# Gate and up columns of an expert's stage moved by one matmul over two runs of 256 columns

## The reference

```python
for e in range(N_EXPERTS):                       # 8
    ye = swiglu(xt, wg[e], wu[e], wd[e])         # (silu(x @ wg) * (x @ wu)) @ wd
    out = out + ye * gates[:, e:e + 1]           # gates: softmax over the top 2, else 0
```

## Time and profile before

| what | value |
| --- | --- |
| median of the timed executions | 1815.68 us (1813.15 to 1816.01) |
| the profiled execution, first to last instruction | 1820.0 us |
| TensorE busy with matmuls | 1738.7 us, 96% |
| VectorE busy | 1251.5 us, 69% |
| ScalarE busy | 983.8 us, 54% |
| mean granted clock of TensorE | 0.954 of full |
| expert part, first stage to last | about 751 to 1805 us |
| load of 1 MB, issue to landing, median | gate 5.2, up 5.3, down 5.0 us |

### The profile page before, as it was taken

How to read it: one execution, slowest core, us unless ns; L and a number is a source line. 1 busy time by engine, 2 the same in 40 slices (tenths; PEclk the granted TensorE clock), 3 DMA queues, 4 the chain that set the end, 5 groups by cost and what they waited for, 6 DMA issues and landing times.

```text
span 1820.0 us, 28008 instructions
## 1 busy us (share of the span) xinstructions
PE 1738.7 (96%) x11045; PEld 1521.8 (84%) x11053; DVE 1251.5 (69%) x1280; ACT 983.8 (54%) x1013; POOL 59.7 (3%) x54
## 2 busy tenths in 40 slices
PE   7998699999899998899999999999999999999998
PEld 5774369999639847899899999899999999999997
DVE  4256655555526543788688888788888888888885
ACT  3344434443145502487577566676676666676664
POOL 0132000000100030100000000000000000000000
PEclk9997589999989999799899999999999999999998
DMA  7321024566204403499899999999999998998993
GB/s 245 93 93 47 1 93 134 167 204 212 93 0 129 148 1 116 139 366 329 282 361 324 324 363 315 327 361 315 332 362 313 335 361 301 349 362 295 352 361 126
DMA packets 335774, 429.10 MB, mean 236 GB/s; under 512 B 9491, under 2 KB 305817, under 8 KB 335409
## 3 DMA queue, kind: packets, MB, share of 16 engines
q1 hardware_dynamic: 332216, 423.77, 69.1%
q10 hardware_dynamic: 3512, 4.73, 0.8%
HBM read 427.43 MB, written 1.05 MB: 235 GB/s over the span
## 4 chain that ended last, share of the span: by engine, by line
PE 84%; DVE 5%; DMA 5%; ACT 3%; issue 2%; SPq 0%; DVEq 0%; ACTq 0%
PE ps L1397 82%; DMA raw<-in_moe_w_up_dram 3%; PE ps L1409 2%; ACT w_hi L825 1%; DMA ring<-in_ffn_w_down_dram 1%; DVE ring_lo L1075 1%; DMA raw<-in_moe_w_down_dram 1%; DVE arena L1021 0%; DVE xg_lo L1330 0%; ACT arena L556 0%; DVE arena L914 0%; DMA arena<-in_meta_tokens_dram 0%; ACT ring_hi L713 0%; DVE arena L1146 0%; SPq L469 0%
## 5 line engine op out<-in xcount | busy, mean ns | idle before, releaser
L1215 DVE TENSOR_TENSOR w_lo<-raw,w_hi 128x2048 fp32r<-128x2048 f32 x336 | 760.9, 2287 | 167.8 <-ACT w_hi L825 164.7
L825 ACT ACTIVATE w_hi<-raw 128x2048 fp32r<-128x2048 f32 x336 | 633.1, 1912 | 29.7 <-DMA raw<-in_moe_w_down_dram 16.2
L1397 PE MATMUL ps<-w_hi,xg_hi 128*128 128x256 f32 x1792 | 517.5, 289 | 2.6 <-DVE xg_lo L1330 2.6
L1397 PE MATMUL ps<-w_hi,xg_lo 128*128 128x256 f32 x1792 | 506.8, 283 | 0.0
L1397 PE MATMUL ps<-w_lo,xg_hi 128*128 128x256 f32 x1792 | 506.8, 283 | 0.0
L1397 PEld LDWEIGHTS ps<-w_hi,xg_hi 128*128 128x128 f32 x1792 | 342.5, 191 | 9.0 <-issue 3.7
L1397 PEld LDWEIGHTS ps<-w_lo,xg_hi 128*128 128x128 f32 x1792 | 343.2, 192 | 3.7
L1397 PEld LDWEIGHTS ps<-w_hi,xg_lo 128*128 128x128 f32 x1792 | 342.7, 191 | 0.0
L850 ACT ACTIVATE eh_hi<-ps 128x256 fp32r<-128x256 f32 x112 | 43.2, 386 | 278.1 <-PE ps L1409 278.1
L1397 PE MATMUL ps<-w_hi,eh_hi 128*128 128x512 f32 x448 | 179.2, 400 | 1.0 <-DVE eh_lo L1302 1.0
L1397 PE MATMUL ps<-w_lo,eh_hi 128*128 128x512 f32 x448 | 177.0, 395 | 0.0
(11 more groups left out here) (244 smaller groups left out, 1954.9 us busy)
## 6 DMA issues: line engine op xcount, KB each, us to landing
raw<-in_moe_w_gate_dram SPq DMA_DIRECT2D x112, 1024.0 KB, 5.2
raw<-in_moe_w_up_dram SPq DMA_DIRECT2D x112, 1024.0 KB, 5.3
raw<-in_moe_w_down_dram SPq DMA_DIRECT2D x112, 1024.0 KB, 5.0
ring<-in_w_in_ab_dram SPq DMA_DIRECT2D x12, 1024.0 KB, 5.4
ring<-in_hy_w_in_dram SPq DMA_DIRECT2D x12, 1024.0 KB, 5.1
ring<-in_ffn_w_gate_dram SPq DMA_DIRECT2D x11, 1024.0 KB, 5.4
ring<-in_ffn_w_up_dram SPq DMA_DIRECT2D x11, 1024.0 KB, 5.4
ring<-in_ffn_w_down_dram SPq DMA_DIRECT2D x8, 1408.0 KB, 7.0
```

What stands on the lines that cost most here:

```text
L825: nc.scalar.activation(w_hi[:, p, at, :], raw[:, p, at, :], ACT.Copy).then_inc(sem(f"{part}_high"), 1)
L1215: V.tensor_tensor(w_lo[:, p, at, :], raw[:, p, at, :], w_hi[:, p, at, :].bitcast(F32), ALU.subtract).then_inc(sem(f"{part}_split"), 1)
L1397: return nc.tensor.matmul(o, l, r, start=start, stop=stop)
```

## The change

`columns`, which did gate or up, gives way to `gate_up(n, p, part)`. One matmul now moves 256 gate columns and the 256 up columns of the same row block, which lie 2048 elements apart in `w_hi` and `w_lo`, and writes all 512 columns of the PSUM bank. Part 0 does the first four of the eight row blocks, part 1 the last four. The turn of the stage before stays in the middle, now between the two parts. Part 0 waits for both `g_split` and `u_split`. One semaphore `gu_used` is raised at the end of part 1, where there were `g_used` after gate and `u_used` after up; the loads of gate and of up, and the silu, wait for it.

```diff
-                    sp.wait_ge(sem(f"{part}_used"), 14 * i + 2 * q + p - 1)
+                    sp.wait_ge(sem("d_used" if part == "d" else "gu_used"), 14 * i + 2 * q + p - 1)
...
             def silu(n, p):
-                act.wait_ge(sem("u_used"), n + 1)
+                act.wait_ge(sem("gu_used"), n + 1)
...
-            def columns(part, n, p):
-
-                pe.wait_ge(sem(f"{part}_split"), n + 1)
-                at = "gud".index(part)
-                w = [a[:, p, at, :].rearrange("p (k n) -> p k n", k=KT) for a in (w_hi, w_lo)]
-                for k in range(KT):
-                    last = product(ps[p][:, 256 * at:256 * at + 256], xg_hi[:, k, :], xg_lo[:, k, :], [a[:, k, :] for a in w], k == 0, k == KT - 1)
-                last.then_inc(sem(f"{part}_used"), 1)
+            def gate_up(n, p, part):
+
+                if part == 0:
+                    pe.wait_ge(sem("g_split"), n + 1)
+                    pe.wait_ge(sem("u_split"), n + 1)
+                w = [a[:, p, 0:2, :].rearrange("p a (k n) -> p a k n", k=KT) for a in (w_hi, w_lo)]
+                for k in range(4 * part, 4 * part + 4):
+                    last = product(ps[p][:, :].rearrange("p (a n) -> p a n", a=2), xg_hi[:, k, :], xg_lo[:, k, :],
+                                   [a[:, :, k, :] for a in w], k == 0, k == KT - 1)
+                if part:
+                    last.then_inc(sem("gu_used"), 1)
...
             def step(n, p):
-                columns("g", n, p)
+                gate_up(n, p, 0)
                 turn_hidden(n - 1, 1 - p)
-                columns("u", n, p)
+                gate_up(n, p, 1)
                 down(n - 1, 1 - p)
```

More of the change, by code:

```diff
@@ L1799, in item @@
                 pe.wait_ge(sem("xg_split"), 2 * i + 2)
-                columns("g", 14 * i, 0)
-                columns("u", 14 * i, 0)
+                gate_up(14 * i, 0, 0)
+                gate_up(14 * i, 0, 1)
                 if not first:
@@ L1807, in item @@
                     add_result(i, 1)
-                columns("g", 14 * i + 1, 1)
+                gate_up(14 * i + 1, 1, 0)
                 turn_hidden(14 * i, 0)
-                columns("u", 14 * i + 1, 1)
+                gate_up(14 * i + 1, 1, 1)
                 if not first:
```

## The result

The changed kernel takes 1928.89 us (median of four, 1926.06 to 1932.07) against 1815.17 us before: the ratio is 1.063, 95% interval 1.062 to 1.065. That is +113.7 us, where +110 and 1926 us were forecast. The changed kernel's profiled execution has a span of 1930.2 us.

A forecast was written before the change was run, and what follows sets the result against it. TensorE was taken to bound the kernel at 8.71 us a stage. Adding 121 us inside items, -10 between them and -1 at entry and end gave +110 on 1815.7: 1926 us, range 1908 to 1948.

The forecast's parts named there:

- TensorE's own work: Gate and up matmuls on TensorE: 24 of 512 columns replace 48 of 256, saving 0.26 us a stage.
- The ring: Turn, high parts, low parts, part 0, next turn: a closed round of 10.11 us instead of 8.71, +1.40 a stage.
- The eighty steady intervals: Turn to turn inside items, ten per item: 8.71 us becomes 10.11, +1.40 each.
- the eight with the extra turns: One interval per item, holding two extra turns: 8.95 us becomes 10.11, the extra turns falling into the new wait.
- Between items: Three intervals around each change of item, where TensorE is the bound: -1.4 us, seven times, -10 us.
- Entry and end: Entry into the first item and end of the last: about -1 us together.
- The loads: Loads of gate, up and down, issued later: 9.06 us for three fits in 10.11, so off the path.
- rival 1: Low parts stay covered and only TensorE's shorter list counts: -29 us, 1787 us; chance 3%.
- rival 2: Load queue sets the stage at 9.06 us, 3.02 per load: +28, 1844 us; chance 4%.
- rival 3: TensorE's clock falls from idling 1.56 us a stage: 2168 us, or 1950 to 2050 if in some stages; chance 6%.
- rival 4: Moving operand in two runs costs double, part 0 takes 5.5 us: +242, 2168 us; chance 3%.

The follow-up runs named there:

- e6: Changed kernel with loads, splits and releases grouped by row halves of both matrices, each part waiting for its own half: 1789.84 us against 1812.84 us before, ratio 0.986.
- e7: The kernel by row halves, with each merged matmul made as two of 256 columns: 1814.07 us against 1814.23 us for the kernel before, ratio 1.000.
- e1: Kernel before the change, with one edit: gate of a stage also waits for u_split; matmuls and load releases stay separate: 1936.37 us, ratio 1.068.
- e3: Changed kernel with the turn after six of the eight row blocks instead of four: 2158.77 us, ratio 1.190.
- e9: Changed kernel with the turn after five of the eight row blocks instead of four: 2033.56 us, ratio 1.120.
- e8: Changed kernel with ScalarE making gate's high part of stage n + 2 ahead of turned_high of stage n: 1868.02 us, ratio 1.032.
- e5: Kernel before the change, with gate's loads released together with up's at the end of up: 1817.49 us against 1812.84 us, ratio 1.003.
- e4: Changed kernel with the turn of the stage before moved ahead of part 0: 1884.05 us, ratio 1.039.
- e10: Changed kernel with the turn after two of the eight row blocks instead of four: 1874.48 us, ratio 1.034.

## Why the prediction was right

**TensorE's own work.** 0.26 us a stage was forecast as saved. e6 against e7 has 8.71 - 8.42 = 0.29 us; the new matmul costs 0.228 us, as taken. Correct, and hidden in the changed kernel.

**The ring.** 7.26 us from turn to part 0, measured 7.28; 10.11 us from turn to turn, measured 10.12. The eighty steady intervals went from 696.9 to 809.7 us, +112.8 (+112 forecast), and the eight with the extra turns from 71.5 to 81.0, +9.5 (+9.3 forecast). e1 shows that the wait suffices, e3 and e9 that part 0 counts in full where the clock held (11.47 and 10.80 us, 11.48 and 10.80 expected), and e8 that ScalarE's order is a link.

**Between items.** The seven groups of three intervals went from 253.2 to 239.2 us, -14.0 where -10 was forecast; 4.4 us of this is one stretch at half clock in the execution before (21.73 us in place of 17.37), which was known from the earlier trace rows and not taken into this term. Entry and end were forecast with -1 and are +2: the first interval grew by 4.8 us, from 9.18 to 14.01, the last one got 0.8 us shorter, and the experts' first turn came some 2 us earlier. In that first interval the loads of stage 2 go out only when gate and up of stage 0 are through (755.91 us), up's high part starts at 764.06 us, TensorE waits 3.49 us, and the clock fell there for 3.4 us. I had added nothing for that. Together 112.8 + 9.5 - 14.0 + 1.9 = 110.2 us between the two profiled executions, where 110 was forecast: the ring is right to 1 us, but that the total is as near as this is luck, since 4 us too little gain between items and 3 us too little loss at the entry cancel.

**The loads.** They were off the path as forecast: up lands in 7.7 us, down in 7.9, ScalarE waits 12.6 us in all for up, and e5 prices the joint release at some 5 us (2 to 9).

**The rivals.** The cover did not hold (rival 1); e6 shows what it would have been worth, 1790 us against 1787 forecast. The load queue (rival 2) did not bind in the changed kernel, and its price was too high: the loads of e6 sustain 3 MB in 8.60 us, 2.87 us each and not 3.02. What binds in e4, e8 and e10, at 9.3 to 9.5 us, is the way of a buffer through load, splits and use, as their chains show. The clock (rival 3) fell in some stages with waits of 2.1 and 2.8 us and in no steady stage with 1.4. Two runs (rival 4) cost no more than one.

## What to carry to other kernels

When two waits are joined into one, ask how late the later was allowed to be: here up's low parts were ready 1.29 us after the start of gate, under cover of gate. Then look whether what is now waited for hangs itself on something later in the same list; if so, it is a ring, its length is every stage's length, and a shorter engine list gains nothing. To merge instructions over two operands without joining their waits, cut load, split and release along the merged instruction and not along the operands: that turned +6.3% into -1.4%. Then look what the shorter stage asks of the loads: here it is already 0.2 us a stage more than they give, and in an item with many more stages the gain would shrink from 0.29 towards 0.11 us a stage (8.71 - 8.60; an estimate from e6, no run has such an item).

## What the runs showed of the hardware

A matmul in a row of matmuls costs 0.120 us at 256 columns and 0.228 at 512. So 256 columns more cost 0.108 us, and some 0.012 us of each matmul do not depend on its columns; two runs of 256 in one instruction pay that once (e6 against e7, 0.29 us for 24 matmuls). Loads of 0.5 and 1 MB in steady supply moved 366 GB/s, 3 MB in 8.60 us: asked for 373 GB/s, they fell behind from stage to stage (e6). TensorE's clock held through a wait of 1.4 us in every steady stage. It fell in 26 of 88 stages that had 2.1 us, and in 62 of 88 that had 2.8 us, which adds 1.6 us to such a stage.
